# The first two weight tiles behind four LayerNorms are multiplied by the un-normalised input

## The chip, the cores and the metric

The kernel runs on one core of a Trainium2 chip. The time is that of one execution on the device, in microseconds (us); the median of three runs stands for the kernel. TensorE multiplies, VectorE, ScalarE and GpSimd (POOL in the profile) do the elementwise work, SyncE (SP) issues the loads of the weights.

## The reference, cut to what matters

A model of two blocks in fp32: 512 positions, width 1024. The first block has two layers of attention and FFN; the second starts with a LayerNorm, and each of its two layers is a token mixer, a LayerNorm, a convolutional FFN and a LayerNorm. What is computed around the change:

```python
def layer_norm(x, g, b):
    mu = jnp.mean(x, axis=-1, keepdims=True)
    var = jnp.mean(jnp.square(x - mu), axis=-1, keepdims=True)
    return (x - mu) * lax.rsqrt(var + EPS) * g + b

def conv_ffn(h, w_up, w_dw, w_down):
    u = depthwise_conv(h @ w_up, w_dw)
    g, val = jnp.split(u, 2, axis=-1)
    return (jax.nn.silu(g) * val) @ w_down

def token_mixers(h, ...):
    proj = h @ w_in          # 20 tiles of 128 columns here
    ...                      # short convolution, gated linear attention (a scan), latent attention, 31-tap convolution
    return y @ w_out
```

`h` in `h @ w_up` and `h @ w_in` is the output of a LayerNorm. Four of the five LayerNorms of the second block are followed by such a product.

## The kernel before

Activations lie transposed, 128 channels on the partitions by 512 positions, so the hidden state is eight slices `h[k]` of 128x512. To keep fp32 precision every product is three matmuls on rounded operands (`gemm`): `whi`·`n_hi` (L668), `whi`·`n_lo` (L669) and `wlo`·`n_hi` (L670). A tile is 128 output channels: eight slices of three matmuls for an input of 1024. Weights stream in: SyncE loads a tile into `raw`; ScalarE makes `whi` (`split_hi`, L639), GpSimd `wlo` = raw - whi (`split_lo`, L559). There are two result banks `bank_G`, two places each of `raw`, `whi` and `wlo`. ScalarE empties a bank (`take`, L645) and right behind it splits the tile two ahead, since that place is free then. So an engine that takes tile n late also lets tile n+2 start late.

The LayerNorms are objects of class `Norm`, `NORMS[0]` to `[4]`; the first four are "split", which means that their result is needed as `n_hi` and `n_lo` for a product. They stand behind the tile groups `down1b` (n = 0, "plain", a last RMS norm is folded in), `out2b` (1), `down2b` (2) and `out3b` (3). 0 and 2 lead into the mixer's input tiles `mix_in`, 1 and 3 (`narrow`) into the FFN's `up2a` and `up3a`. Behind each tile of the group VectorE adds the residual, subtracts a rough mean ("shift", L919), and ScalarE squares. `norm_tile_pe` sums over channels with matmuls by a matrix of ones: the first moment into `bank_O` (L792, the last part L827), the second into `bank_S` (L795, L829). Each call is two passes. When the last part is in, `norm_end_act` squares the mean (L864), takes Ln (L866) and Exp (L868), which gives the scale `rstd`; `norm_end_dve` centres the slices (L952), forms the variance (L966), and goes over the eight slices: norm (L977), centre of a slice four ahead, `n_lo` of the slice before (L956). ScalarE makes `n_hi` (L878) and adds the bias to `h` (L873).

TensorE starts the next group by `ramp_gemms_n`: the first two tiles slice by slice as each `n_lo` arrives, the second two slices behind; then `ramp_next_n`, the third tile in halves, whose halves of `whi` and `wlo` are made by themselves (L621, L627, L609, L612). In the FFN, VectorE then convolves gate and up (L1103, L1104, L1105 each), multiplies (`prod`, L1125) and makes `a_lo` (L1127), ScalarE applies silu (L1082) and makes `a_hi` (L1084), one chunk of a gate and an up tile at a time; `take` of the gate waits for the convolution of the chunk before, `take` of up for its product. In the mixer, tiles 0 and 1 and two small matmuls (AUP) feed the decay chain: `gate_in` (L2517, L2736), Exp and Ln (L2521, L2522), L2741, two scans (L2744), and then decays (L2269 to L2272), 31 taps (L2756) and mask copies (L2295) on VectorE, between which TensorE goes through the input tiles and, at L2221, the scan's matmuls. The order on each engine is the order of the code; engines meet only at semaphores.

## Time and profile before

| | us |
|---|---|
| median of 3 runs (2587.82 to 2592.54) | 2589.61 |
| the profiled execution | 2590.14 |
| its span | 2588.2 |
| TensorE busy | 2481.5 |
| VectorE busy | 1719.8 |
| ScalarE busy | 1024.9 |
| GpSimd busy | 958.2 |

The span is the time from the first to the last instruction that the profiler saw; 1.9 us of the profiled execution lie around it. The mean granted clock of TensorE over the span is 0.985 of full. Busy shares are means over the span; where an engine stands still, and for whom, is told by the rows below.

### The profile page before, as it was taken

What the parts mean: (1) busy time and instruction counts of PE and PEld (TensorE: products, weight loads), DVE (VectorE), ACT (ScalarE), POOL (GpSimd) and SP (SyncE); (2) the same over time, 40 slices, a digit from 0 to 9 for tenths busy, and PEclk for the clock granted to TensorE, in tenths of its full rate; (3) what the DMA queues carried; (4) which work ended last, traced back from release to release, by engine and by line L of the source; (5) the groups of instructions that cost most, each with busy time, mean ns of one, the idle gap of its engine ahead of it and who ended that gap; (6) DMA issues with size and microseconds to landing.
All of it is one profiled execution on the core that took longest, in us unless ns stands there. A gap on an engine that the chain in (4) does not pass through costs nothing.

```text
span 2588.2 us, 33451 instructions
## 1 busy us (share of the span) xinstructions
PE 2481.5 (96%) x11222; PEld 1907.6 (74%) x11222; DVE 1719.8 (66%) x2281; ACT 1024.9 (40%) x1623; POOL 958.2 (37%) x391
## 2 busy tenths in 40 slices
PE   7999999999999999999899889999989988999997
PEld 5676787888777688888676467788767746778876
DVE  7654774587777777276787667718668755781875
ACT  4444432232344532123554644313345454431333
POOL 2222444444310044444263034444435403453452
PEclk9999999999999999999999999999999999999999
DMA  5212232232332223223222022322322202232222
GB/s 171 78 58 61 86 97 90 89 100 95 102 92 74 74 89 101 90 94 106 67 90 62 13 66 85 105 86 89 104 77 83 66 8 74 81 98 89 94 97 77
DMA packets 65342, 217.48 MB, mean 84 GB/s; under 512 B 8416, under 2 KB 8672, under 8 KB 65120
## 3 DMA queue, kind: packets, MB, share of 16 engines
q1 hardware_dynamic: 64384, 214.79, 25.8%
q10 hardware_dynamic: 864, 1.44, 0.2%
q8 instruction: 58, 0.95, 0.2%
q14 instruction: 36, 0.29, 0.0%
HBM read 207.81 MB, written 2.10 MB: 81 GB/s over the span
## 4 chain that ended last, share of the span: by engine, by line
PE 78%; DVE 9%; issue 6%; ACT 3%; POOL 2%; DMA 0%; DVEq 0%; SPq 0%; ACTq 0%; POOLq 0%
PE bank_G L668 23%; PE bank_G L670 23%; PE bank_G L669 23%; POOL wlo L559 2%; DVE conv_up L1105 2%; DVE prod L1125 1%; ACT whi L639 1%; DVE h L952 1%; PE bank_S L1705 1%; PE bank_S L2221 1%; PE bank_X L1733 1%; PE bank_O L1957 1%; PE bank_O L1719 1%; PE bank_S L1946 1%; DVE conv_up L1104 1%
## 5 line engine op out<-in xcount | busy, mean ns | idle before, releaser
L559 POOL TENSOR_TENSOR wlo<-raw,whi 128x1024 fp32r<-128x1024 f32 (+2 forms) x361 | 905.3, 2509 | 1518.1 <-ACT whi L639 1493.0
L668 PE MATMUL bank_G<-n_hi,whi 128*128 128x512 f32 x2248 | 903.8, 402 | 49.3 <-DVE n_lo L956 27.2
L669 PE MATMUL bank_G<-n_lo,whi 128*128 128x512 f32 x2248 | 880.9, 392 | 0.0
L670 PE MATMUL bank_G<-n_hi,wlo 128*128 128x512 f32 x2248 | 880.8, 392 | 0.0
L639 ACT ACTIVATE whi<-raw 128x1024 fp32r<-128x1024 f32 (+2 forms) x389 | 403.4, 1038 | 603.8 <-PE bank_G L670 603.6
L668 PEld LDWEIGHTS bank_G<-n_hi,whi 128*128 128x128 f32 x2248 | 425.3, 189 | 168.7 <-DVE n_lo L956 36.3
L670 PEld LDWEIGHTS bank_G<-n_hi,wlo 128*128 128x128 f32 x2248 | 425.3, 189 | 91.3
L669 PEld LDWEIGHTS bank_G<-n_lo,whi 128*128 128x128 f32 x2248 | 425.9, 189 | 88.2 <-issue 4.8
L668 PE MATMUL bank_G<-a_hi,whi 128*128 128x512 f32 x704 | 277.9, 395 | 9.1 <-DVE a_lo L1127 3.9
L669 PE MATMUL bank_G<-a_lo,whi 128*128 128x512 f32 x704 | 275.2, 391 | 0.0
L670 PE MATMUL bank_G<-a_hi,wlo 128*128 128x512 f32 x704 | 275.0, 391 | 0.0
L668 PEld LDWEIGHTS bank_G<-a_hi,whi 128*128 128x128 f32 x704 | 132.8, 189 | 42.6 <-DVE a_lo L1127 7.3
L1105 DVE SCALAR_TENSOR_TENSOR conv<-gate,vec,conv 128x512 f32<-128x512 f32 x88 | 147.4, 1675 | 13.4 <-DVE conv L1104 7.6
L669 PEld LDWEIGHTS bank_G<-a_lo,whi 128*128 128x128 f32 x704 | 132.9, 189 | 28.0 <-issue 0.7
L670 PEld LDWEIGHTS bank_G<-a_hi,wlo 128*128 128x128 f32 x704 | 132.9, 189 | 27.9
L1024 DVE SCALAR_TENSOR_TENSOR h<-h,bank_G 128x512 f32 x32 | 21.9, 687 | 190.6 <-PE bank_G L670 190.6
L1887 DVE TENSOR_TENSOR h<-h,bank_G 128x512 f32<-128x512 f32 x80 | 54.9, 686 | 137.0 <-PE bank_G L670 136.9
L1125 DVE TENSOR_TENSOR prod<-silu,up 128x512 f32<-128x512 f32 x44 | 112.8, 2564 | 35.8 <-ACT silu L1073 35.8
L1105 DVE SCALAR_TENSOR_TENSOR conv_up<-up,vec,conv_up 128x512 f32<-128x512 f32 x44 | 112.6, 2559 | 6.4
L1127 DVE TENSOR_TENSOR a_lo<-prod,a_hi 128x512 f32 x88 | 60.9, 692 | 80.2 <-ACT a_hi L1084 40.1
L1101 DVE TENSOR_SCALAR conv<-gate,vec 128x512 f32<-128x512 f32 x44 | 98.1, 2229 | 10.2 <-DVE gate L655 10.2
L1104 DVE SCALAR_TENSOR_TENSOR conv<-gate,vec,conv 128x512 f32<-128x512 f32 x88 | 92.2, 1048 | 13.4 <-DVE conv L1101 7.0
(333 smaller groups left out, 2681.9 us busy)
## 6 DMA issues: line engine op xcount, KB each, us to landing
raw<-in_w_mix_in SPq DMA_DIRECT2D x40, 512.0 KB, 3.3
raw<-in_w_hyb_in SPq DMA_DIRECT2D x25, 512.0 KB, 3.4
raw<-in_w_diff_in SPq DMA_DIRECT2D x24, 512.0 KB, 3.3
raw<-in_w_up0a SPq DMA_DIRECT2D x22, 512.0 KB, 3.3
raw<-in_w_up0b SPq DMA_DIRECT2D x22, 512.0 KB, 3.3
raw<-in_w_up1a SPq DMA_DIRECT2D x22, 512.0 KB, 3.3
raw<-in_w_up1b SPq DMA_DIRECT2D x22, 512.0 KB, 3.3
raw<-in_w_up2a SPq DMA_DIRECT2D x22, 512.0 KB, 3.3
```

The source lines that it names most:

```text
L559: pool.tensor_tensor(b.wlo[:, g.slot, w], b.raw[:, g.slot, w], b.whi[:, g.slot, w], ALU.subtract).then_inc(b.lo_ready, 1)
L639: act.activation(b.whi[:, g.slot, w], b.raw[:, g.slot, w], ACT.Copy).then_inc(b.hi_ready, 1)
L668: pe.matmul(out, b.whi[:, g.slot, w], hi[:, hi_at + k, :], start=(k == 0), stop=False)
L669: pe.matmul(out, b.whi[:, g.slot, w], lo[:, lo_at + k, :], start=False, stop=False)
L670: mm = pe.matmul(out, b.wlo[:, g.slot, w], hi[:, hi_at + k, :], start=False, stop=(k == pieces - 1))
L952: dve.scalar_tensor_tensor(h[k], b.O[:, 0, :], -1.0 / D, h[k], ALU.mult, ALU.add).then_inc(b.centred, 1)
L1101: link(dve.tensor_scalar(dst[:, :], src[:, s:s + T], v_(b, w, c), v_(b, bias, c), ALU.mult, ALU.add))
L1104: link(dve.scalar_tensor_tensor(dst[:, :], src[:, s + 1:s + 1 + T], v_(b, w, FC + c), dst[:, :], ALU.mult, ALU.add))
L1105: return dve.scalar_tensor_tensor(dst[:, :], src[:, s + 2:s + 2 + T], v_(b, w, 2 * FC + c), dst[:, :], ALU.mult, ALU.add)
L1125: dve.tensor_tensor(b.prod[:, :], b.silu[:, :], up, ALU.mult).then_inc(b.prod_done, 1)
L1127: dve.tensor_tensor(b.a_lo[:, bass.ds(i, 1), :].rearrange("p a t -> p (a t)"), b.prod[:, :], b.a_hi[:, bass.ds(i, 1), :].rearrange("p a t ...
L1887: dve.tensor_tensor(h, h, b.G[:, g.slot, :], ALU.add).then_inc(b.evacuated, 1)
```

## The change

Normalising is linear: with x the shifted, un-normalised state, W'(((x - m)·s)·g + b) = s·(W'(x·g) - m·W'g) + W'b. The first two tiles (`EARLY = 2`) behind each split LayerNorm are now multiplied by x·g, before the moments are known, and corrected afterwards. The parts:

- ScalarE copies x·gain as `early_hi` behind each slice's square, VectorE makes the low half (L1073), in the tiles of the group before; they lie in buffers of their own (`early_ffn`, `early_mix`).
- TensorE forms W'g and W'b by a matmul with two moving columns, gain and bias, and the raw fp32 weights as the stationary operand (L892), eight for each early tile: those of the first inside the last product of the group, those of the second inside the first early tile. The moment matmuls go between the slices of the first early tile (`norm_sums_pe`).
- The scale is written to `bank_S` in PSUM, not to `rstd`. The rough mean is read from PSUM by VectorE without a copy by ScalarE.
- ScalarE copies the sums to `wcol`, makes mean × W'g for both tiles (L981) and adds W'b at the end (L986); VectorE adds the bank and multiplies by the scale (L1117, L1119), behind the second and the fifth norm. The low halves come two slices behind the norm, not one.
- The ramp is made of tiles 2 and 3, and tile 4 is the one in halves. `take` of tile 2 waits for the first convolution, of tile 3 for the first product (`after_early`).
- In the mixer the AUP matmuls come before the ramp, the bias copies of `gate_in` among the `n_hi`; the takes of tiles 2 and 3 stand ahead of the Exp and Ln of the decay chain. The mixer's small weights are loaded on ScalarE's queue before the last down group, not at the mixer's start.

```diff
+def early_split_lo(pool, b, name, m):
+    if m == 1:
+        pool.wait_ge(b.shifted, 8 * RAMPS.index(name) + 8)
+    if m == 2 * EARLY:
+        ramp_lo(pool, b, name)
+    else:
+        split_lo(pool, b, Index(FIRST[name] + m), W8)
...
-    g0 = FIRST[name]
+    g0 = FIRST[name] + EARLY
...
         self.shifts = {3: (0, 1, 2), 4: (3, 4)} if self.narrow else {3: (0, 1, 2, 3), 4: (4,)}
         self.shifts |= {5: (5,), 6: (6,), 7: (7,)}
+        self.lows = {4: (0,), 5: (1, 2), 6: (3,)} if self.narrow else {4: (0, 1), 5: (2, 3), 6: (4, 5)}
+        self.lows |= {7: range(4 if self.narrow else 6, KD)}
...
+def norm_sums_pe(pe, b, x, step):
+    if x.narrow:
+        if step == 0:
+            pe.wait_ge(b.shift_summed, x.added("q3"))
+            moment_pe(pe, b, x, 1, b.ntmp[:, 0])
+            pe.wait_ge(b.shift_summed, x.added("q5"))
+            moment_pe(pe, b, x, 0, b.rstd[:, :])
+        if step == 1:
+            moment_pe(pe, b, x, 1, b.ntmp[:, 1])
+            pe.wait_ge(b.shifted, 8 * x.n + 7)
+            moment_pe(pe, b, x, 0, b.h[:, 6, :])
+        if step == 2:
+            pe.wait_ge(b.shift_squared, 8 * x.n + 7)
+            moment_pe(pe, b, x, 1, b.mixed[:, 1])
+    elif step == 1:
+        if x.plain:
+            pe.wait_ge(b.plain_summed, 6)
+            pe.matmul(b.O[:, 1, :], b.k["ones"], b.mixed[:, 1], start=True, stop=False)
+        pe.wait_ge(b.shift_summed, x.added("q6"))
+        moment_pe(pe, b, x, 0, b.acc[:, :], True)
+        moment_pe(pe, b, x, 1, b.mixed[:, 0], True)
+    if step != 3:
         return
...
     pe.wait_ge(b.shifted, 8 * x.n + 8)
-    pe.matmul(b.O[:, 0, :], b.k["ones"], b.h[:, 7, :], start=False, stop=True).then_inc(b.first_moment, 1)
+    moment_pe(pe, b, x, 0, b.h[:, 7, :], stop=True).then_inc(b.first_moment, 1)
     pe.wait_ge(b.shift_squared, 8 * x.n + 8)
-    pe.matmul(b.S[:, 1, :], b.k["ones"], square_at(b, x, 7), start=False, stop=True).then_inc(b.second_moment, 1)
+    moment_pe(pe, b, x, 1, square_at(b, x, 7), stop=True).then_inc(b.second_moment, 1)
...
+def gain_sums_pe(pe, b, x, j, part):
+    g = Index(FIRST[x.ramp] + j)
+    for k in part:
+        if k == 0:
+            pe.wait_ge(loaded_at(b, g), loaded_count(g))
+            if j == 0:
+                free_bank(pe, b, x.w_at)
+                wait(pe, b.w_taken, x.n)
+        mm = pe.matmul(b.X[:, x.w_at.slot, 2 * j:2 * j + 2], b.raw[:, g.slot, k * P:(k + 1) * P], x.gain_and_bias(b, k),
+                       start=(k == 0), stop=(k == KD - 1))
+        if k == KD - 1:
+            mm.then_inc(b.w_summed, 1)
+def last_product_after(pe, b, x, pieces):
+    per = -(-KD // pieces)
+    return lambda k: gain_sums_pe(pe, b, x, 0, range(min(KD, k * per), min(KD, (k + 1) * per)))
+def early_pe(pe, b, x):
+    g0, (hi, lo) = FIRST[x.ramp], x.early(b)
+    def after(k):
+        gain_sums_pe(pe, b, x, 1, range(k, k + 1))
+        norm_sums_pe(pe, b, x, k)
+    gemm(pe, b, Index(g0), hi, lo, KD, lambda k: pe.wait_ge(b.early_lo, KD * x.n + k + 1), after=after)
+    gemm(pe, b, Index(g0 + 1), hi, lo, KD)
 def norm_products_pe(pe, b, x, hi, lo, pieces, ready):
     for m in range(KD):
-        gemm(pe, b, Index(x.g0 + m), hi, lo, pieces, ready if m == 0 else None)
-        norm_tile_pe(pe, b, x, m)
+        last = x.split and m == KD - 1
+        gemm(pe, b, Index(x.g0 + m), hi, lo, pieces, ready if m == 0 else None,
+             after=last_product_after(pe, b, x, pieces) if last else None)
+        norm_part_pe(pe, b, x, m)
+    if x.split:
+        early_pe(pe, b, x)
...
+        if x.split:
+            act.activation(x.early(b)[0][:, k, :], b.h[:, k, :], ACT.Copy, scale=v_(b, x.gain, k)).then_inc(b.early_hi, 1)
+def scale_of(b):
+    return b.S[:, 0, :]
...
     act.wait_ge(b.first_moment, n + 1)
     act.activation(b.acc[:, :], b.O[:, 0, :], ACT.Square, scale=1.0 / D).then_inc(b.moment_squared, 1)
+    if x.split:
+        act.wait_ge(b.centred, 8 * n + AHEAD[0])
+        act.activation(b.mean[:, :], b.O[:, 0, :], ACT.Copy, scale=-1.0 / D).then_inc(b.mean_taken, 1)
     act.wait_ge(b.variance_ready, n + 1)
     act.activation(b.rstd[:, :], b.rstd[:, :], ACT.Ln, bias=b.zero if x.plain else b.eps2).then_inc(b.scale_ready, 1)
     act.wait_ge(b.scale_ready, 2 * n + 1)
-    act.activation(b.rstd[:, :], b.rstd[:, :], ACT.Exp, scale=-0.5).then_inc(b.scale_ready, 1)
+    act.activation(scale_of(b), b.rstd[:, :], ACT.Exp, scale=-0.5).then_inc(b.scale_ready, 1)
+    if x.split:
+        act.wait_ge(b.w_summed, EARLY * (n + 1))
+        sums = b.X[:, x.w_at.slot, 0:2 * EARLY]
+        act.activation(b.wcol[:, 0:EARLY], sums[:, 0:2 * EARLY:2], ACT.Copy)
+        act.activation(b.wcol[:, EARLY:], sums[:, 1:2 * EARLY:2], ACT.Copy).then_inc(b.w_taken, 1)
+        act.wait_ge(b.w_taken, n + 1)
+        for j in range(EARLY):
+            act.activation(x.first_tile(b, j), b.mean[:, :], ACT.Copy, scale=b.wcol[:, j:j + 1]).then_inc(b.early_mean, 1)
+    def early_take(j):
+        y = x.first_tile(b, j)
+        act.wait_ge(b.early_tmp, 2 * (EARLY * n + j + 1))
+        act.activation(y, y, ACT.Identity, bias=b.wcol[:, EARLY + j:EARLY + j + 1]).then_inc(b.evacuated, 1)
...
+            if k == 0:
+                early_take(0)
+                split_hi(act, b, Index(FIRST[x.ramp] + EARLY))
+            if k == 3:
+                split_hi(act, b, Index(FIRST[x.ramp] + EARLY + 1))
+            if k == 4:
+                early_take(1)
+            if k == 5 and not x.narrow:
+                gate_copies_act(act, b, n // 2)
             if k >= 2:
                 biased(k - 2)
         else:
...
-        dve.tensor_tensor(h[k], h[k], b.mean[:, :], ALU.subtract).then_inc(b.shifted, 1)
+        dve.scalar_tensor_tensor(h[k], b.S[:, 0, :], -1.0 / (2 * P), h[k], ALU.mult, ALU.add).then_inc(b.shifted, 1)
...
+    if x.split:
+        for k in x.lows.get(m, ()):
+            dve.wait_ge(b.early_hi, KD * n + k + 1)
+            dve.scalar_tensor_tensor(x.early(b)[1][:, k, :], h[k], v_(b, x.gain, k), x.early(b)[0][:, k, :], ALU.mult,
+                                     ALU.subtract).then_inc(b.early_lo, 1)
...
         centre(k)
+    def norm(k):
+        dve.wait_ge(b.centred, 8 * n + k + 1)
+        dve.scalar_tensor_tensor(h[k], h[k], v_(b, x.gain, k), scale_of(b), ALU.mult, ALU.mult).then_inc(b.normed, 1)
+    def correct(j):
+        g, y = Index(FIRST[x.ramp] + j), x.first_tile(b, j)
+        dve.wait_ge(b.early_mean, EARLY * n + j + 1)
+        dve.wait_ge(b.gemm_done, g.n + 1)
+        dve.tensor_tensor(y, y, b.G[:, g.slot, :], ALU.add).then_inc(b.early_tmp, 1)
+        dve.wait_ge(b.early_tmp, 2 * (EARLY * n + j) + 1)
+        dve.tensor_tensor(y, y, scale_of(b), ALU.mult).then_inc(b.early_tmp, 1)
+    if x.narrow:
+        for y in (b.gate, b.up):
+            dve.memset(y[:, 0:PAD], 0.0).then_inc(b.padded, 1)
+            dve.memset(y[:, PAD + T:], 0.0).then_inc(b.padded, 1)
     dve.wait_ge(b.scale_ready, 2 * n + 2)
     for k in range(KD):
-        dve.wait_ge(b.centred, 8 * n + k + 1)
-        dve.scalar_tensor_tensor(h[k], h[k], v_(b, x.gain, k), b.rstd[:, :], ALU.mult, ALU.mult).then_inc(b.normed, 1)
+        norm(k)
         if k + AHEAD[1] < KD:
             centre(k + AHEAD[1])
-        if x.split and k:
-            low(k - 1)
+        if not x.split:
+            continue
+        if k == 1:
+            correct(0)
+        if k == 4:
+            correct(1)
+        if k >= 2:
+            low(k - 2)
     if x.split:
+        low(KD - 2)
         low(KD - 1)
...
+    def after_early():
+        act.wait_ge(b.conv_done, c0 + 1)
+        take(act, b, Index(g0 + 2), b.gate[:, PAD:PAD + T], ramp=True)
+        act.activation(b.silu[:, :], b.conv[:, :], ACT.Silu).then_inc(b.silu_done, 1)
+        act.wait_ge(b.prod_done, c0 + 1)
+        take(act, b, Index(g0 + 3), b.up[:, PAD:PAD + T], width=W8)
+        act.activation(b.a_hi[:, 0, :], b.prod[:, :], ACT.Copy).then_inc(b.act_hi, 1)
+        act.wait_ge(b.conv_done, c0 + 2)
+        act.activation(b.silu[:, :], b.conv[:, :], ACT.Silu).then_inc(b.silu_done, 1)
+        act.wait_ge(b.prod_done, c0 + 2)
+        act.activation(b.a_hi[:, 1, :], b.prod[:, :], ACT.Copy).then_inc(b.act_hi, 1)
+    if name in RAMPS:
+        after_early()
...
             free_bank(pe, b, p)
             pe.matmul(b.X[:, p.slot, :], b.aup[rows, :], b.mx[rows, M_GA, :], start=True, stop=True).then_inc(b.posted, 1)
-    ramp_next_n(pe, b, f"mix_in{l}", gate_up)
-    for m in range(3, SCAN_TILE):
+    gate_up()
+    ramp_gemms_n(pe, b, f"mix_in{l}", 48 + 24 * l)
+    ramp_next_n(pe, b, f"mix_in{l}")
+    for m in range(2 * EARLY + 1, SCAN_TILE):
         tile(m)
...
+def mixer_weights_act(act, b, l, mixw):
     if l:
         act.wait_ge(b.headed, HEADS0[3])
+    act.dma_start(b.aup[:, :], mixw[l, :, 10 * P:11 * P]).then_inc(b.mix_w_in, 16)
     act.dma_start(b.uq[:, :, :], mixw[l, :, 0:6 * P].rearrange("p (k m) -> p k m", k=2)).then_inc(b.mix_w_in, 16)
     act.dma_start(b.ukv[:, :], mixw[l, :, 6 * P:10 * P]).then_inc(b.mix_w_in, 16)
...
-        take(act, b, Index(g0 + m), b.mx[:, m, :], GLA_DK ** -0.5 if m == M_GQ else 1.0, ramp=m == 0)
-    act.wait_ge(b.evacuated, g0)
-    tile(0)
-    tile(1)
-    for d in range(2):
...
+        take(act, b, Index(g0 + m), b.mx[:, m, :], GLA_DK ** -0.5 if m == M_GQ else 1.0, ramp=m == EARLY)
+    tile(2)
+    tile(3)
     x = b.gate_in[:, 2:4, :]
     act.wait_ge(b.gate_abs, l + 1)
     link(act.activation(x, x, ACT.Exp, scale=-1.0))
     act.activation(x, x, ACT.Ln, bias=b.one).then_inc(b.gate_log, 1)
-    tile(2)
-    act.wait_ge(b.evacuated, g0 + M_GATE + 2)
+    tile(4)
     for j in range(2):
         y = b.mx[:, M_GATE + j, :]
...
```

TensorE behind the LayerNorm of `out2b`, from the last product of the group. `ntmp`, `rstd`, `h`, `mixed` and `sq` are sources of moment calls, `const` the ones. Before:

```order
L670 MATMUL bank_G<-n_hi,wlo 128x512
L795 MATMUL bank_S<-ntmp,const 128x512
L792 MATMUL bank_O<-rstd,const 128x512
L795 MATMUL bank_S<-ntmp,const 128x512
L792 MATMUL bank_O<-h,const 128x512
L795 MATMUL bank_S<-mixed,const 128x512
L827 MATMUL bank_O<-h,const 128x512
L829 MATMUL bank_S<-sq,const 128x512
L668 MATMUL bank_G<-n_hi,whi 128x512
```

and now:

```order
L892 MATMUL bank_X<-vec,raw 128x2 x2
L694 MATMUL bank_G<-early_ffn_61,whi 128x512
L695 MATMUL bank_G<-early_ffn_62,whi 128x512
L696 MATMUL bank_G<-early_ffn_61,wlo 128x512
L892 MATMUL bank_X<-vec,raw 128x2
L836 MATMUL bank_S<-ntmp,const 128x512
L836 MATMUL bank_O<-rstd,const 128x512
L694 MATMUL bank_G<-early_ffn_61,whi 128x512
L695 MATMUL bank_G<-early_ffn_62,whi 128x512
L696 MATMUL bank_G<-early_ffn_61,wlo 128x512
L892 MATMUL bank_X<-vec,raw 128x2
L836 MATMUL bank_S<-ntmp,const 128x512
```

The calls of the moments, which stood in one row, are now spread over the slices of a tile that works on the early buffers, with the two-column calls between.

VectorE at the end of the same LayerNorm. Before:

```order
L952 SCALAR_TENSOR_TENSOR h<-bank_O,h 128x512
L966 SCALAR_TENSOR_TENSOR rstd<-bank_S,acc 128x512
L952 SCALAR_TENSOR_TENSOR h<-bank_O,h 128x512 x3
L977 SCALAR_TENSOR_TENSOR h<-h,vec,rstd 128x512
L952 SCALAR_TENSOR_TENSOR h<-bank_O,h 128x512
L977 SCALAR_TENSOR_TENSOR h<-h,vec,rstd 128x512
L952 SCALAR_TENSOR_TENSOR h<-bank_O,h 128x512
L956 SCALAR_TENSOR_TENSOR n_lo<-h,vec,n_hi 128x512
L977 SCALAR_TENSOR_TENSOR h<-h,vec,rstd 128x512
L952 SCALAR_TENSOR_TENSOR h<-bank_O,h 128x512
L956 SCALAR_TENSOR_TENSOR n_lo<-h,vec,n_hi 128x512
```

and now:

```order
L1124 MEMSET gate 128x2
L1123 MEMSET up 128x2
L1124 MEMSET up 128x2
L1111 SCALAR_TENSOR_TENSOR h<-h,vec,bank_S 128x512
L1084 SCALAR_TENSOR_TENSOR h<-bank_O,h 128x512
L1111 SCALAR_TENSOR_TENSOR h<-h,vec,bank_S 128x512
L1084 SCALAR_TENSOR_TENSOR h<-bank_O,h 128x512
L1117 TENSOR_TENSOR gate<-gate,bank_G 128x512
L1119 TENSOR_TENSOR gate<-gate,bank_S 128x512
L1111 SCALAR_TENSOR_TENSOR h<-h,vec,bank_S 128x512
L1084 SCALAR_TENSOR_TENSOR h<-bank_O,h 128x512
L1088 SCALAR_TENSOR_TENSOR n_lo<-h,vec,n_hi 128x512
```

The first low half of the normalised slices comes behind the third norm where it came behind the second, and the correction of the gate tile stands ahead of it.

ScalarE at the start of the FFN behind it. Before:

```order
L621 ACTIVATE whi<-raw 128x512
L873 ACTIVATE h<-h,vec 128x512 x2
L645 ACTIVATE gate<-bank_G 128x512
L627 ACTIVATE whi<-raw 128x512
L645 ACTIVATE up<-bank_G 128x512
L639 ACTIVATE whi<-raw 128x1024
L1082 ACT_TABLE_LOAD
L1082 ACTIVATE silu<-conv 128x512
L1084 ACTIVATE a_hi<-prod 128x512
```

and now:

```order
L647 ACTIVATE whi<-raw 128x512
L991 ACTIVATE h<-h,vec 128x512 x2
L671 ACTIVATE gate<-bank_G 128x512
L653 ACTIVATE whi<-raw 128x512
L1248 ACT_TABLE_LOAD
L1248 ACTIVATE silu<-conv 128x512
L671 ACTIVATE up<-bank_G 128x512
L665 ACTIVATE whi<-raw 128x1024
L1251 ACTIVATE a_hi<-prod 128x512
L1253 ACTIVATE silu<-conv 128x512
L1255 ACTIVATE a_hi<-prod 128x512
```

The take of `up` has moved behind the first silu, and the high half of the second chunk's product ahead of the loop.

## Rows read from the trace of the kernel before

**Rows 1.** Page, busy time of the engines, and the costliest group of GpSimd (busy, mean ns)

```profile
PE 2481.5 (96%) x11222; PEld 1907.6 (74%) x11222; DVE 1719.8 (66%) x2281; ACT 1024.9 (40%) x1623; POOL 958.2 (37%) x391
...
L559 POOL TENSOR_TENSOR wlo<-raw,whi 128x1024 fp32r<-128x1024 f32 (+2 forms) x361 | 905.3, 2509 | 1518.1 <-ACT whi L639 1493.0
```

**Rows 2.** Waits of TensorE: us in total, times, longest us

```profile
PE bank_G L668 <- DVE n_lo L956: 27.2, 12, 6.9
```

**Rows 3.** Timeline of TensorE behind `out2b`: start us, us, what [idle before <- releaser]

```profile
1531.02 1.02 PE L795 MATMUL bank_S<-ntmp,const 128*128 128x512 f32 x2
...
1535.31 1.02 PE L827 MATMUL bank_O<-h,const 128*128 128x512 f32 x2
...
1543.39 0.79 PE L668 MATMUL bank_G<-n_hi,whi 128*128 128x512 f32 x1 [6.20 <-DVE n_lo L956]
...
1571.02 0.49 PE L668 MATMUL bank_G<-n_hi,whi 128*128 128x512 f32 x1 [1.46 <-POOL wlo L559]
...
1582.03 0.39 PE L668 MATMUL bank_G<-n_hi,whi 128*128 128x512 f32 x1
```

**Rows 4.** Windows: us, busy of PE, PEld, DVE, ACT, POOL, clock, DMA share, GB/s

```profile
1543.00:1550.00 7.00, 6.06 (x13) 3.84 (x14) 7.00 (x12) 4.79 (x8) 0.00 (x0) 0.50 0.00 0
1440.00:1444.00 4.00, 1.30 (x6) 0.42 (x4) 3.63 (x9) 1.09 (x4) 0.00 (x0) 1.00 0.02 9
1444.00:1450.00 6.00, 3.65 (x5) 1.59 (x6) 3.22 (x8) 3.48 (x8) 0.00 (x0) 0.57 0.00 0
```

**Rows 5.** Timeline of VectorE behind `out2b`, to the product of the FFN's second chunk

```profile
1540.08 0.74 DVE L977 SCALAR_TENSOR_TENSOR h<-h,vec,rstd 128x512 f32<-128x512 f32 x1
...
1551.74 1.63 DVE L956 SCALAR_TENSOR_TENSOR n_lo<-h,vec,n_hi 128x512 fp32r<-128x512 f32 x2
...
1557.52 0.49 DVE L1103 TENSOR_SCALAR conv<-gate,vec 128x512 f32<-128x512 f32 x1 [3.75 <-ACT gate L645]
...
1560.61 2.62 DVE L1103 TENSOR_SCALAR conv_up<-up,vec 128x512 f32<-128x512 f32 x1
...
1565.15 0.69 DVE L1125 TENSOR_TENSOR prod<-silu,conv_up 128x512 f32<-128x512 f32 x1
...
1575.90 0.69 DVE L1125 TENSOR_TENSOR prod<-silu,conv_up 128x512 f32<-128x512 f32 x1
```

**Rows 6.** Timeline of ScalarE, then of GpSimd, at the same place

```profile
1539.15 0.63 ACT L868 ACTIVATE rstd<-rstd 128x512 f32<-128x512 f32 x1
...
1566.90 1.05 ACT L639 ACTIVATE whi<-raw 128x1024 fp32r<-128x1024 f32 x1
...
1560.48 2.47 POOL L559 TENSOR_TENSOR wlo<-raw,whi 128x1024 fp32r<-128x1024 f32 x1 [1.24 <-ACT whi L639]
```

**Rows 7.** The chain that ended last (eight transposes), and TensorE by line (busy, mean ns)

```profile
75.08 1.02 PE bank_X L1733 x8
...
L1914 PE MATMUL bank_S<-lamp,const 64*128 64x2 f32 x2 | 0.4, 258 | 0.0
...
L668 PEld LDWEIGHTS bank_G<-n_hi,whi 128*128 128x128 f32 x2248 | 425.3, 189 | 168.7 <-DVE n_lo L956 36.3
```

**Rows 8.** Timelines of TensorE and VectorE in the first mixer of the second block

```profile
1263.86 1.02 PE L808 MATMUL bank_O<-mixed,const 128*128 128x512 f32 x2
...
1268.20 1.12 PE L827 MATMUL bank_O<-h,const 128*128 128x512 f32 x2 [0.75 <-DVE h L919]
...
1301.24 1.22 DVE L2741 TENSOR_TENSOR gate_in<-gate_in 128x1024 f32<-128x1024 f32 x1 [1.59 <-ACT gate_in L2522]
...
1305.95 0.50 PE L668 MATMUL bank_G<-n_hi,whi 128*128 128x512 f32 x1 [1.43 <-POOL wlo L559]
...
1308.20 2.61 DVE L2270 TENSOR_TENSOR decayed<-ntmp 128x256 f32<-128x256 f32 x1
...
1349.47 1.34 DVE L2295 COPY_PREDICATED scores_t<-glmask,bank_X 128x512 f32<-128x512 uint8 x2
...
1350.95 0.38 PE L2221 MATMUL bank_S<-const 32*128 32x128 f32 x2
```

166 lines of the change are left out of this document (92 added, 74 removed).

## The prediction

> **What bounds the kernel now.** I read the page first: TensorE is busy for 2481.5 us of the 2588.2 us span, VectorE for 1719.8 us [rows 1]. Little can be won but where TensorE stands still, so the next view is that of its waits. Its longest from one cause is on `n_lo` ahead of a tile, 27.2 us over 12 waits, the longest 6.9 us [rows 2]: four LayerNorms, each with one long and some short waits. The timeline of TensorE around one of them (behind `out2b`) has the pattern [rows 3]. The last product of the group ends where the first moment matmul starts, at 1531.02; I call this E. The last part of the first moment starts at 1535.31, 4.3 us later, and the next tile only at 1543.39, after 6.20 us of idling. In the windows view the idling has a sequel: from 1543 to 1550 TensorE is granted 0.50 of its clock (1.2 GHz, half of 2.4) [rows 4]. The place thus costs 6.20 us, and half of the 7 us at half clock, 3.5 us. Over four places that would be 39 us, the most that the change could bring if TensorE alone set the end. It does not do so here: behind the LayerNorm, VectorE's convolution [rows 5] and the loop take, weight split, product [rows 6] go on without slack. So I follow VectorE and ask when it comes to its next piece of the chain.
>
> **FFN places (LN behind `out2b` and `out3b`), step by step from E.**
>
> *TensorE to the first moment.* Before: E+4.3. After, in program order: 8 two-column calls ahead of E's end, then four early slices of three matmuls, four two-column calls, five moment calls. A slice is .68 us and a moment call .86, since those before start at 1531.02 and 1535.31 with five between the two [rows 3]. No two-column call of 128 rows by raw fp32 weights is in the trace. The nearest are the fp32 transposes, 8 in 1.02 us, .13 each, and a 64-row call of two, 258 ns for both, .13 each [rows 7]. The calls take two passes each. I take .13 a pass, .26 a call; the bounds are 0 (wholly hidden beside the neighbours) and .19 a pass, the mean of a weight load of the products [rows 7]. The sum is 8 × .26 + 4 × (.68 + .26) + 5 × .86 = 2.1 + 3.8 + 4.3 = 10.2 us. First moment at E+10.2 where it was E+4.3: **+5.9 us**.
>
> A page weighs on this price by a sentence that my sum does without: the Trainium skill, "TensorE: Matmul & The Clock Gate", section "LDWEIGHTS (loading the stationary operand)", lets a load of 128 columns cost about 107 ns at any number of moving columns; by that, an estimate, 24 passes ahead of the moment would make the place 0.55 us cheaper.
>
> *To the first norm.* The chain square, variance, Ln, Exp, norm took from 1535.31 by Exp at 1539.15 to the norm at 1540.08 [rows 3, 5, 6], 4.8 us. It stays, with four memsets (.5 us) and the wait for ScalarE's copy of the mean (some .1) ahead of the first norm: about 1546.6.
>
> *VectorE's own work.* Before, 8 norms, 4 centres and 8 low halves took from 1540.08 to 1553.37, 13.3 us for 20 instructions, .66 each [rows 5]. After, four correction instructions join (.62 each, like the .69 us products of [rows 5], 2.5 us), inside that row. Now a new neighbour: GpSimd's split of the third tile's `wlo`, which waits for ScalarE's `whi` behind the first `n_hi`, falls from about 1552.1 to 1554.6 into the low halves. Beside such a split (2.47 us, at 1560.48) VectorE's L1103 took 2.62 us instead of .49 [rows 5, 6], 2.1 more. I count one such stretch, at 1.8 us, since part of the split lies beside a norm. Sum 13.3 + 2.5 + 1.8 = 17.6, less .2 since it overlaps the end: last low half at 1564.0, **+10.6 us** against 1553.4. Bounds of the stretch: 0 and 2 × 2.1.
>
> The Trainium skill, "SBUF — State Buffer", on the port pair that VectorE and GpSimd share, has an operation with two SBUF inputs fully blocked by a GpSimd read, and one with at most one (the other in PSUM) free. By that the low halves are stretched, while the norms, whose scale now lies in PSUM, are not; no row of before has a low half beside GpSimd. If it doesn't hold for them, the sum is 1.8 us less a place, 2594.
>
> *What the early tiles give back.* Before, VectorE then waited 3.75 us for the gate tile, and its first convolution began at 1557.52 and the product at 1565.15, 7.6 us later, the stretched L1103 (2.1 us too long) among it [rows 5]. After, both tiles of chunk 0 lie corrected in SBUF, so it begins at once, at 1564.0; only splits of half a tile lie beside it, for which I put .4 in place of the 2.1, 5.9 us: product at **1569.9, +4.8 us**. Chunk 1: its gate is taken before the product, but `up` only behind it; then `a_hi`, a low half stretched by GpSimd, and the convolution: second product 1579.7 against 1575.9, **+3.8 us**. Only then does ScalarE free the bank of the seventh tile, split its weights (1.05 us [rows 6]) and GpSimd the low half (2.5 us [rows 1]): the tile starts at 1585.1 against 1582.03 [rows 3], **+3.0 us**. From there each chunk of two tiles follows the last in the same loop as before, whose links (take, split, low split, product) leave TensorE no room to catch up; the shift stays to the end of the group.
>
> *TensorE meanwhile.* It works from E through two early tiles to 1552.4, idles 2.5 us and again 2.7 us (low halves), and is ahead at its fifth tile, 1568.2 against 1571.02 [rows 3]; but then it idles about 5 us before the seventh. A clock of 0.57 followed 4 us of which TensorE was busy for 1.30 [rows 4], and 0.50 followed the 6.20. If the 5 us have that sequel, it costs up to 3.5 us more. So +3 without, +6.5 with it; I take the middle: **+4.5 us each, +9 for both**.
>
> **Mixer places (LN behind `down1b` and `down2b`).** From E=1263.86 the last part of the first moment started 4.3 us later, at 1268.20 [rows 8]; after, 2.1 + 3.8 and four other calls of .86 with no gap between, E+9.2: +4.9. TensorE's fifth tile was at 1305.95 [rows 8] and comes at about 1300.0, −6. But the mixer's decay chain on VectorE starts with L2741 at 1301.24 [rows 8] after ScalarE's Exp and Ln. These stand now behind the takes of tiles 2 and 3; the last of them is at 1300.4, and L2741 comes at 1304.1: **+2.9**. What VectorE owes from here is the bound: its four mask copies end at 1350.81, and the scan matmuls that read them start at 1350.95 [rows 8]. TensorE's lead of 6 us ends there. Against the +2.9: some instructions of 256 columns took 2.6 us, L2270 at 1308.20 among them, where 1024 columns took 1.22 [rows 8]; they lay beside GpSimd's splits, which come earlier now. Two may come free, some 4.4 us. Bounds −1.5 and +3; I take **+1 each, +2 for both**.
>
> **Hidden at no price.** The mean shift without its ScalarE copy and the early halves on ScalarE (8 × .7 us) and VectorE (8 × .66, half of them ahead of E) go beside the last products. If they are late, TensorE waits in the early slices (case D). The mixer's weight DMAs move from the mixer's start to before the last down group: aup is wanted tens of us later. GpSimd's first early tile has its split before E; the second waits for the last shift, as before.
>
> **Sum.** 9 + 2 = +11 us on the profiled 2590.14 us gives 2601.1; the median is .5 lower, 2589.61: I say **2601.0**. At 0 a pass it is 4 × 3.1 less (2589), at .19 a pass 4 × 1.4 more (2607); without the stretches 4 × 1.8 less.
>
> **Rivals.**
> - *A, the forecast:* own range 2590 to 2614, chance .58, of which .16 lies within 0.2%.
> - *B1, TensorE's lead is kept throughout* (faster). If chunk loops and scan have slack that I do not see, each place gives its lead: 2 × 3 and 2 × 6 us, 2572. For it: TensorE 96% busy [rows 1]. Against: the convolution waits for its tile and the scan matmuls start .14 us behind the mask copies [rows 5, 8]. Decides if VectorE reaches the mask copies 2.9 us or more before TensorE. .08.
> - *B2, the lead is kept in the mixers alone:* 2 × −6 + 2 × 3 = −6, 2584. The escape from GpSimd speaks for it. .16 (.12 faster, .04 same).
> - *C, gaps with sequel in the clock, at all four places:* 2 × 6.5 + 2 × (2.9 + 3.5) = +26, 2616. .10.
> - *D, it doesn't do what it says:* the early low halves, four of them behind the last shift on VectorE (2.6 us), hold TensorE and so the moments: +2.6 each on A, 2611. .08.
>
> **Numbers.** 0.2% is 5.2 us, about what a measurement of this kernel can tell. Faster .08 + .12 = .20; same .16 + .04 = .20; slower .42 + .10 + .08 = .60. From 2582 to 2614 B1 and most of C are left out, under .2; the ends take in the prices of a pass.
>
> **What would show it.** In the profile after: two-column calls at a pitch of .26; the last moment part at E+10; no idle of 6 us before the first tile but gaps of 2.5 us at the third; the last `n_lo` 10 us later; the product of chunk 0 near E+39, of chunk 1 near E+49; a gap of 5 us before the seventh tile; L2741 3 us later against E. Wrong it would be if TensorE's seventh tile starts earlier against E than before, if the granted clock stays 1.00, or if the scan matmuls start earlier.

## The result, and the profile after

| | before | after |
|---|---|---|
| median, us | 2589.90 (2587.82 to 2592.54) | 2614.58 (2609.39 to 2618.33) |
| profiled execution, us | 2590.14 | 2617.62 |
| its span, us | 2588.2 | 2615.8 |

The ratio is 1.0108, with a 95% interval from 1.0081 to 1.0134: slower by 24.7 us. I had said 2601.0, with 2614.0 as the upper end. The sign was right, the size (11.4 us) was less than half of what came. The kernel before is itself spread: in later sessions its executions took 2579 to 2593 us, with a mean of 2585 to 2587, so the profiled one, 2590.14, lies near their upper end, and the profiled one of after lies 3.0 us above its median.

Where it went can be read without a model. Both kernels issue the same 9240 product matmuls (L668 to L670 before, L694 to L696 after) in the same order. Take the n-th of each and subtract its start from that of before: the difference is the lag. Read in quiet stretches between the places, it is -1.2 us ahead of the first LayerNorm, +5.1 behind the first mixer, +12.1 behind the FFN, +22.1 behind the second mixer and +27.7 behind the second FFN. So the four places cost **+6.3, +7.0, +9.9 and +5.6 us**: the two mixers 16.2, the two FFNs 12.6. This compares one execution with one other.

The page, and the waits of TensorE (us in total, times, longest):

```profile
PE 2497.6 (95%) x11350; PEld 1925.8 (74%) x11350; DVE 1761.6 (67%) x2329; ACT 1048.2 (40%) x1670; POOL 966.4 (37%) x391
...
PE bank_G L694 <- POOL wlo L576: 24.8, 29, 5.1
...
PE bank_S L2400 <- DVE scores_t L2474: 9.0, 5, 2.9
...
PE bank_G L694 <- DVE n_lo L1088: 7.6, 4, 2.3
...
PE bank_S L2400 <- ACT scores_t L2425: 5.6, 2, 2.9
```

The wait on `n_lo` fell from 27.2 to 7.6 us [rows 2], so the change does what it says. But GpSimd's low halves are now waited for up to 5.1 us at a time, and the waits of the scan matmuls on VectorE's mask copies and on ScalarE's copies (both write `scores_t`) are new.

**The FFN place behind `out2b`.** TensorE first, then VectorE and GpSimd, timeline of the kernel after (start us, us, what [idle before <- releaser]); the last product's end, E, is 1536.0, which is 1537.79, the start of the first early slice, less eight two-column calls of .22:

```profile
1535.14 0.50 PE L892 MATMUL bank_X<-vec,raw 128*128 128x2 f32 x4
1535.51 0.47 PE L694 MATMUL bank_G<-n_hi,whi 128*128 128x512 f32 x1
1535.82 0.39 PE L695 MATMUL bank_G<-n_lo,whi 128*128 128x512 f32 x1
...
1545.74 1.10 PE L836 MATMUL bank_O<-h,const 128*128 128x512 f32 x2
...
1558.94 0.47 PE L694 MATMUL bank_G<-n_hi,whi 128*128 128x512 f32 x1 [2.12 <-issue]
...
1562.86 0.79 PE L694 MATMUL bank_G<-n_hi,whi 128*128 128x512 f32 x1 [1.60 <-DVE n_lo L1088]
...
1591.22 0.79 PE L694 MATMUL bank_G<-n_hi,whi 128*128 128x512 f32 x1 [5.07 <-POOL wlo L576]
```

```profile
1550.79 0.74 DVE L1111 SCALAR_TENSOR_TENSOR h<-h,vec,bank_S 128x512 f32<-128x512 f32 x1
...
1556.54 0.75 DVE L1111 SCALAR_TENSOR_TENSOR h<-h,vec,bank_S 128x512 f32<-128x512 f32 x1
...
1557.80 1.60 DVE L1088 SCALAR_TENSOR_TENSOR n_lo<-h,vec,n_hi 128x512 fp32r<-128x512 f32 x1
...
1566.03 2.06 DVE L1088 SCALAR_TENSOR_TENSOR n_lo<-h,vec,n_hi 128x512 fp32r<-128x512 f32 x3
...
1575.51 0.69 DVE L1299 TENSOR_TENSOR prod<-silu,conv_up 128x512 f32<-128x512 f32 x1 [2.22 <-ACT silu L1248]
...
1585.37 0.69 DVE L1299 TENSOR_TENSOR prod<-silu,conv_up 128x512 f32<-128x512 f32 x1
...
1556.49 2.35 POOL L576 TENSOR_TENSOR wlo<-raw,whi 128x1024 fp32r<-128x1024 f32 x1 [13.83 <-ACT whi L665]
```

The windows over the gap and behind it (us, busy of PE, PEld, DVE, ACT, POOL, granted clock, DMA share, GB/s):

```profile
1584.00:1590.00 6.00, 2.15 (x10) 1.45 (x8) 4.61 (x7) 3.49 (x5) 1.69 (x1) 1.00 0.00 0
1590.00:1596.00 6.00, 4.78 (x11) 3.79 (x12) 5.65 (x4) 0.63 (x1) 3.86 (x2) 0.53 0.43 125
```

| from E, us | before [rows 3, 5] | forecast | after |
|---|---|---|---|
| last part of the first moment | 4.3 | 10.2 | 9.7 |
| first norm | 9.1 | 15.6 | 14.8 |
| last low half ready | 22.4 | 33.0 | 32.1 |
| product of chunk 0 | 34.1 | 38.9 | 39.5 |
| product of chunk 1 | 44.9 | 48.7 | 49.4 |
| seventh tile | 51.0 | 54.1 | 55.2 |

The working of this place held step by step to about 1 us, with the 5 us gap ahead of the seventh tile and the granted clock of 0.53 (nearer 1.2 GHz than 2.4) behind it.

The price of the place was still above the forecast, and the reason lies further up than the seventh tile. TensorE had idled 2.12 us ahead of its third tile, and its clock fell there too. The third tile therefore ended late, ScalarE's take of it waited 3.14 us on TensorE, the first silu stood behind this take and a table load, and VectorE waited 2.22 us for the silu. In e12 below, whose code is the same here, the clock was down for a shorter time, the take waited for VectorE and not for TensorE, and VectorE did not wait for the silu (its product began at 1569.66, when the silu had ended at 1569.56). ScalarE's take and the windows behind the first gap, first in the kernel after, then in e12, where E is 4.7 us earlier:

```profile
1572.41 0.60 ACT L671 ACTIVATE gate<-bank_G 128x512 f32<-128x512 f32 x1 [3.14 <-PE bank_G L696]
...
1561.00:1564.00 3.00, 1.40 (x4) 0.95 (x4) 3.00 (x4) 1.92 (x4) 1.26 (x1) 0.50 0.42 119
1564.00:1567.00 3.00, 3.00 (x10) 2.33 (x9) 3.00 (x6) 3.00 (x6) 0.00 (x0) 0.59 0.40 146
...
1566.50 0.60 ACT L671 ACTIVATE gate<-bank_G 128x512 f32<-128x512 f32 x1 [1.91 <-DVE conv L1279]
...
1554.00:1557.00 3.00, 2.73 (x6) 1.84 (x6) 2.97 (x5) 2.62 (x5) 1.97 (x2) 0.53 0.47 175
1557.00:1560.00 3.00, 1.99 (x9) 1.51 (x9) 3.00 (x4) 2.29 (x4) 0.58 (x1) 0.90 0.38 102
```

The lag of the seventh tile within the place is +4.1 us in the kernel after and +3.0 in e12; one tile later it is +7.0 and +4.5.

**The first mixer.** VectorE, then GpSimd and TensorE, timeline of the kernel after (here E is 1263.4: the start of the last tile of `down1b` and the length that this tile had before, so that the two-column calls inside it count as after E):

```profile
1305.23 1.33 DVE L2914 TENSOR_TENSOR gate_in<-gate_in 128x1024 f32<-128x1024 f32 x1 [6.29 <-ACT gate_in L2698]
...
1317.75 2.58 DVE L2451 TENSOR_TENSOR const<-ntmp 128x256 f32<-128x256 f32 x1
1320.55 5.35 DVE L2945 TENSOR_TENSOR cpad<-mx 128x512 f32<-128x512 f32 x2 [0.22 <-DVE const L2451]
...
1339.79 2.60 DVE L2449 TENSOR_TENSOR decayed<-ntmp 128x256 f32<-128x256 f32 x1
...
1354.54 1.33 DVE L2474 COPY_PREDICATED scores_t<-glmask,bank_X 128x512 f32<-128x512 uint8 x2
...
1317.67 2.37 POOL L576 TENSOR_TENSOR wlo<-raw,whi 128x1024 fp32r<-128x1024 f32 x1 [6.38 <-ACT whi L665]
1320.01 2.56 POOL L2673 TENSOR_TENSOR decayed<-decayed,mx 128x1024 f32<-128x1024 f32 x1
1322.52 2.82 POOL L576 TENSOR_TENSOR wlo<-raw,whi 128x1024 fp32r<-128x1024 f32 x1
...
1346.30 0.38 PE L2400 MATMUL bank_S<-const 32*128 32x128 f32 x2 [2.73 <-ACT scores_t L2425]
```

L2914, the old L2741, comes at E+41.8 where it came at E+37.4 [rows 8]. The first four mask copies end at E+92.4, where they ended at E+86.9. GpSimd now goes from one instruction into the next for four instructions from 1317.67 on, and both `cpad` products lie beside it: 5.35 us for two. In the kernel before only one of the two lay beside GpSimd (2.77 us). In this mixer 6 instructions of VectorE of some 2.6 us stand where there were 3, in the second one 9 where there were 4. Each of these 22 ends 0.28 to 0.55 us behind the end of a GpSimd instruction beside it, which is why I call them collisions. The second mixer shows what follows; TensorE at five scan matmuls, some 10 us apart:

```profile
2008.95 0.38 PE L2400 MATMUL bank_S<-const 32*128 32x128 f32 x2 [2.88 <-ACT scores_t L2425]
...
2018.82 0.38 PE L2400 MATMUL bank_S<-const 32*128 32x128 f32 x2 [1.45 <-DVE scores_t L2474]
...
2028.63 0.38 PE L2400 MATMUL bank_S<-decayed 32*128 32x128 f32 x2 [2.95 <-DVE scores_t L2474]
...
2037.43 0.58 PE L2400 MATMUL bank_S<-decayed 32*128 32x128 f32 x2 [1.95 <-DVE scores_t L2474]
...
2047.20 0.38 PE L2400 MATMUL bank_S<-const 32*128 32x128 f32 x2 [1.33 <-DVE scores_t L2474]
```

None of these waits is there in the kernel before. I call such a row a cascade.

### The profile page after: what moved, and what is told of

Same layout as the page of the kernel before. It is cut to its first block, busy times and chain, and to the rows that moved or that the text cites. A ratio compares the mean times of both kernels' runs of the same rounds, so it can differ in the third digit from the quotient of the medians.

```text
span 2615.8 us, 33724 instructions
## 1 busy us (share of the span) xinstructions
PE 2497.6 (95%) x11350; PEld 1925.8 (74%) x11350; DVE 1761.6 (67%) x2329; ACT 1048.2 (40%) x1670; POOL 966.4 (37%) x391
## 4 chain that ended last, share of the span: by engine, by line
PE 74%; DVE 13%; issue 7%; ACT 3%; POOL 2%; DVEq 1%; DMA 0%; ACTq 0%; POOLq 0%; SPq 0%
PE bank_G L694 22%; PE bank_G L696 21%; PE bank_G L695 21%; POOL wlo L576 2%; DVE conv_up L1279 2%; ACT whi L665 1%; DVE prod L1299 1%; PE bank_S L1884 1%; PE bank_X L1912 1%; DVE h L1084 1%; PE bank_O L2136 1%; PE bank_O L1898 1%; PE bank_S L2125 1%; DVE n_lo L1088 1%; DVE bank_O L2929 1%
## 5 line engine op out<-in xcount | busy, mean ns | idle before, releaser
L694 PE MATMUL bank_G<-n_hi,whi 128*128 128x512 f32 x2184 | 881.5, 404 | 46.7 <-POOL wlo L576 21.2
L696 PE MATMUL bank_G<-n_hi,wlo 128*128 128x512 f32 x2184 | 858.5, 393 | 0.0
L695 PE MATMUL bank_G<-n_lo,whi 128*128 128x512 f32 x2184 | 858.0, 393 | 0.0
L694 PEld LDWEIGHTS bank_G<-n_hi,whi 128*128 128x128 f32 x2184 | 414.9, 190 | 159.5 <-issue 41.6
L696 PEld LDWEIGHTS bank_G<-n_hi,wlo 128*128 128x128 f32 x2184 | 414.5, 190 | 89.6
L695 PEld LDWEIGHTS bank_G<-n_lo,whi 128*128 128x128 f32 x2184 | 415.5, 190 | 86.7 <-issue 5.1
L694 PE MATMUL bank_G<-a_hi,whi 128*128 128x512 f32 x704 | 279.0, 396 | 9.9 <-DVE a_lo L1301 3.9
L696 PE MATMUL bank_G<-a_hi,wlo 128*128 128x512 f32 x704 | 274.8, 390 | 0.0
L694 PEld LDWEIGHTS bank_G<-a_hi,whi 128*128 128x128 f32 x704 | 132.6, 188 | 43.2 <-DVE a_lo L1301 7.2
L696 PEld LDWEIGHTS bank_G<-a_hi,wlo 128*128 128x128 f32 x704 | 132.5, 188 | 28.0
L1275 DVE TENSOR_SCALAR conv<-gate,vec 128x512 f32<-128x512 f32 x44 | 98.1, 2229 | 10.2 <-DVE gate L681 10.2
```

The source lines that it names most:

```text
L694: pe.matmul(out, b.whi[:, g.slot, w], hi[:, hi_at + k, :], start=(k == 0), stop=False)
L695: pe.matmul(out, b.whi[:, g.slot, w], lo[:, lo_at + k, :], start=False, stop=False)
L696: mm = pe.matmul(out, b.wlo[:, g.slot, w], hi[:, hi_at + k, :], start=False, stop=(k == pieces - 1))
L1275: link(dve.tensor_scalar(dst[:, :], src[:, s:s + T], v_(b, w, c), v_(b, bias, c), ALU.mult, ALU.add))
```

## The experiments

The places of all runs, as lags between the same matmuls, in the one execution that was profiled; "long" is the number of VectorE instructions of 1.9 to 3 us (mask copies and scans left out) in the two mixers; "chain" is the start of L2741 or L2914 after E. Some expectations put a place or E by up to 2 us otherwise (4.7 and 9.5 us for the two mixers of the kernel after, E+42.5 for its chain); the table reads all runs in one way. The ratio is to the kernel before, from all timed runs.

| run | mixer 1 | FFN 1 | mixer 2 | FFN 2 | long | chain | ratio (95%) |
|---|---|---|---|---|---|---|---|
| before | 0 | 0 | 0 | 0 | 3, 4 | 37.4, 34.9 | 1 |
| after | +6.3 | +7.0 | +9.9 | +5.6 | 6, 9 | 41.8, 39.5 | 1.0108 (1.0081 to 1.0134) |
| e1 | +3.5 | +4.6 | +1.1 | +4.2 | 5, 5 | 37.6, 35.3 | 1.0068 (1.0052 to 1.0085) |
| e2 | +7.8 | +3.4 | +9.2 | +3.0 | 7, 9 | 41.4, 37.7 | 1.0101 (1.0077 to 1.0125) |
| e3 | +14.9 | +2.7 | +6.2 | +2.8 | 10, 7 | 41.9, 39.9 | 1.0065 (1.0048 to 1.0082) |
| e4 | +3.1 | +3.2 | +2.4 | +2.8 | 5, 5 | 40.3, 39.5 | 1.0106 (1.0084 to 1.0128) |
| e5 | +3.6 | -0.1 | +6.6 | 0.0 | 5, 7 | 37.6, 33.8 | 1.0020 (1.0006 to 1.0035) |
| e6 | +0.4 | -1.9 | -2.5 | +0.2 | 3, 4 | 40.2, 36.8 | 1.0006 (0.9993 to 1.0019) |
| e7 | +3.2 | +2.6 | +0.3 | +2.7 | 5, 5 | 37.6, 35.2 | 1.0054 (1.0035 to 1.0073) |
| e8 | +3.5 | -0.8 | -0.3 | -0.6 | 5, 5 | 37.5, 33.8 | 1.0025 (1.0012 to 1.0038) |
| e9 | -1.5 | +0.1 | -5.0 | +0.1 | 3, 3 | 37.6, 33.8 | 0.9999 (0.9985 to 1.0013) |
| e10 | -1.3 | 0.0 | -5.1 | +0.2 | 3, 3 | 37.6, 33.8 | 1.0008 (0.9991 to 1.0025) |
| e11 | 0.0 | 0.0 | -0.1 | 0.0 | 3, 4 | 37.4, 34.9 | 1.0000 (0.9986 to 1.0013) |
| e12 | +0.3 | +4.4 | -2.1 | +4.2 | 2, 3 | 41.8, 39.5 | 1.0042 (1.0024 to 1.0061) |
| e13 | +0.3 | +3.2 | -3.6 | +2.9 | 2, 3 | 41.8, 39.5 | 1.0031 (1.0017 to 1.0046) |
| e14 | -1.2 | +7.0 | -4.1 | +5.7 | 3, 3 | 37.6, 35.2 | 1.0041 (1.0021 to 1.0061) |
| e15 | +0.5 | -1.0 | -5.0 | -0.5 | 3, 3 | 37.6, 33.8 | 0.9979 (0.9968 to 0.9990) |

How far can one execution mislead? e11 gives 0.0, 0.0, -0.1 and 0.0, but e6 has -1.9 in the first FFN, where its code is that of the kernel before: the granted clock over the 22 us from E was 0.84 in e6 and 0.77 in the kernel before.

```profile
1531.00:1553.00 22.00, 15.25 (x39) 8.77 (x38) 17.17 (x27) 14.16 (x20) 4.65 (x2) 0.77 0.15 48
...
1528.00:1550.00 22.00, 15.25 (x46) 8.90 (x45) 16.79 (x26) 13.74 (x20) 4.66 (x2) 0.84 0.15 48
```

My theory at the start was that ScalarE's order delays VectorE's decay chain in the mixer, and that the late moment and the clock make the FFN's price. The rival in the mixer was that only the collisions of VectorE with GpSimd count.

**e1, ScalarE's Exp and Ln first.**

```diff
-    tile(2)
-    tile(3)
     x = b.gate_in[:, 2:4, :]
     act.wait_ge(b.gate_abs, l + 1)
     link(act.activation(x, x, ACT.Exp, scale=-1.0))
     act.activation(x, x, ACT.Ln, bias=b.one).then_inc(b.gate_log, 1)
+    tile(2)
+    tile(3)
```

> Against the changed kernel, whose first mixer place costs 4.7 us and the second 9.5 by the trace. Edit: in the mixer, ScalarE's Exp and Ln of the decay gates stand ahead of the takes of tiles 2 and 3. Theory (ScalarE's order delays VectorE's decay chain): L2914 comes 3.5 to 4 us earlier against E, the scan matmuls too, at both places, so 7 to 8 us less: some 2607. Rival (what sets the end of the scan is how often VectorE lies beside GpSimd's splits): L2914 earlier by the same, but the scan matmuls by less than 1.5 us, total within 3 us of 2614.6. Third case: the later takes of tiles 2 and 3 hold TensorE at tiles 4 and 5; then the time is the same or longer.

The chain came 4.2 us earlier at both places and the time fell by 0.40%, 10 us, more than either expectation. But the masks of the first mixer ended only 2.5 us earlier (E+89.9), and the number of long instructions fell as well, so this run does not part the two theories.

**e2, the moments first.**

```diff
-    def after(k):
-        gain_sums_pe(pe, b, x, 1, range(k, k + 1))
-        norm_sums_pe(pe, b, x, k)
+    for step in range(4):
+        norm_sums_pe(pe, b, x, step)
+    gain_sums_pe(pe, b, x, 1, range(KD))
...
-        if k == 1:
+        if k == 3:
             correct(0)
-        if k == 4:
+        if k == 6:
             correct(1)
```

> Edit: all moment matmuls stand ahead of the first early slice, the two-column sums of the second early tile right behind them, and the two corrections come behind the fourth and seventh norm (takes and splits on ScalarE moved with them). Theory (the late moment is what delays VectorE): last part of the first moment at E+6.1 instead of E+9.7 behind out2b, last low half 3.5 us earlier against E, and all four places cheaper by about 3.5: some 2600. Rival (VectorE's and GpSimd's later work would be late anyhow, or the early tile now arrives too late for the correction): last low half earlier by less than 1.5 us, or a new wait of VectorE on bank_G ahead of the correction, total 2610 to 2615.

The last part of the first moment came at 1543.21, 6.1 us after E, and both FFN places fell by about 3 us (7.0 to 3.4, 5.6 to 3.0). In the mixers it did nothing: 7 and 9 long instructions, cascade and all. A miss for "all four places".

**e3, silu first.**

```diff
         act.wait_ge(b.conv_done, c0 + 1)
-        take(act, b, Index(g0 + 2), b.gate[:, PAD:PAD + T], ramp=True)
         act.activation(b.silu[:, :], b.conv[:, :], ACT.Silu).then_inc(b.silu_done, 1)
+        take(act, b, Index(g0 + 2), b.gate[:, PAD:PAD + T], ramp=True)
         act.wait_ge(b.prod_done, c0 + 1)
-        take(act, b, Index(g0 + 3), b.up[:, PAD:PAD + T], width=W8)
         act.activation(b.a_hi[:, 0, :], b.prod[:, :], ACT.Copy).then_inc(b.act_hi, 1)
+        take(act, b, Index(g0 + 3), b.up[:, PAD:PAD + T], width=W8)
```

> Edit: at the start of the FFN behind a split LayerNorm, ScalarE's first silu (with its table load) stands ahead of the take of tile 2, and the first a_hi ahead of the take of tile 3. Theory (VectorE's waits of 2.2 us on silu and 2.3 us on a_hi are handed on to the seventh tile): product of chunk 0 2 us earlier, of chunk 1 3 us earlier, seventh tile 3 us earlier, 6 us less in all: some 2609. Rival (the later take of tile 2 delays the second half of tile 4, and the gap before tile 7 only moves): seventh tile within 1 us, total within 2 us.

The seventh tile's lag in the place fell from 4.1 to 1.3 us, as expected; about 1.1 us of that is the clock behind the first gap, since e1, e4 and e12, without this edit, have 3.0. The mixers, whose code is that of the kernel after, cost +14.9 and +6.2 in this trace, against +6.3 and +9.9: with the same instructions they vary by many microseconds, and so does the number of their long instructions. The traced execution, 2618.12 us, was the slowest of five; the other four took 2599 to 2603.

**e4, TensorE kept busy ahead of the seventh tile.**

```diff
         gemm_n(pe, b, Index(g0 + 2 * EARLY + 1))
+        for _ in range(19):
+            pe.matmul(b.S[:, 1, :], b.n_hi[:, 0, 0:P], b.n_hi[:, 1, :], start=True, stop=True)
         done = 2 * EARLY + 2
```

> Edit: 19 extra matmuls (128x512, sources n_hi, result unused) stand on TensorE ahead of the seventh tile in the two FFNs behind a split LayerNorm, where it idles for 5.1 us; 19 x .2265 = 4.3 us, so that they end before the tile may start. Their result is used by nothing. Theory (the gap lowers the granted clock, and that costs 3 us a place): the clock stays at 1.00 after the seventh tile's start, seventh tile at the same time against E, 12th matmul behind it 3 us earlier, 5 to 6 us less in all: some 2609. Rival (the clock falls for another reason, or the loop's links on VectorE take back what the clock gives): clock down in the same stretch, or up and the total within 2 us of 2614.6.

The granted clock behind the seventh tile stayed at 1.00 and the FFN places cost 3.2 and 2.8. The total did not show it. The traced execution, 2601.66 us, was the fastest of four (the others 2607 to 2616), so its mixers, +3.1 and +2.4, do not speak for the others; that the mixers took the rest is argued, not shown.

**e5, e1 to e3 together; e7, e1 and e3; e8, e5 with the matmuls of e4.**

> The three edits of e1, e2 and e3 together on the changed kernel. Behind out2b the seventh tile started 4.1 us later against E in the changed kernel, 1.3 later with the moments first, 1.2 later with silu first. If the two act on the same chain (product of chunk 0 and 1 on VectorE), both add: seventh tile 1.5 us earlier than before, each FFN place at -1 to +1. Mixers: decay chain (L2914) at about E+36 at the first, where before had E+37.4, 4 or fewer stretched instructions of VectorE, no row of gaps; place 0 to +2. Total within 5 us of before. Rival (the corrections on VectorE, 2.5 us a place, cannot be won back by any order): FFN places stay at +2 to +3, mixers +2 to +4, total 8 to 12 us above before.

> The edits of e1 and e3 together on the changed kernel, moments left where the change put them. Theory (they act at different places and add): FFN places +2.7 each, mixer places +1 to +4 each, total 8 to 13 us above before. Rival (a cascade of gaps in the mixer depends on where VectorE stands against GpSimd, not on this order): a mixer place of +6 or more.

> e5 with the 19 extra matmuls of e4 ahead of the seventh tile (their result is used by nothing). If a gap of over 3 us stands there in e5 and the clock falls behind it, this is 1 to 3 us a place faster than e5. If the gap in e5 is shorter than the 4.3 us that they take, they delay the seventh tile by the difference and the total is 0 to 4 us longer than e5.

The FFN edits add, as expected: -0.1 and 0.0 in e5. Its mixers missed: +3.6 and +6.6 with 5 and 7 long instructions, where I had expected 0 to +2 with 4 or fewer. In e7 the FFN places came as expected (2.6 and 2.7), the total 14 us above before and not 8 to 13. The extra matmuls gave 0.7 and 0.6 us a place, below what was expected, and e5 and e8 have the same ratio within their intervals. In e5 the second mixer had a cascade (+6.6), in e8 with the same code none (-0.3).

**e6, the late chain alone, in the kernel before.**

```diff
+    tile(2)
+    link(act.activation(x, x, ACT.Copy))
     link(act.activation(x, x, ACT.Exp, scale=-1.0))
     act.activation(x, x, ACT.Ln, bias=b.one).then_inc(b.gate_log, 1)
-    tile(2)
```

> The kernel BEFORE with nothing of the change, but in the mixer ScalarE takes tile 2 and makes one extra copy of gate_in onto itself ahead of the Exp and Ln of the decay gates, so that VectorE's chain (L2741) starts some 4 us later against E, as in the changed kernel. Theory (the mixer places cost what they do since this chain is late, and lateness brings further collisions of VectorE with GpSimd and waits of TensorE): both mixer places cost 4 to 10 us, gaps of 2 to 3 us on TensorE at the scan matmuls, total 2596 to 2606. Rival (the cost comes from the early tiles and corrections themselves): each place costs less than 2 us, total within 4 us of before.

My theory fell. The chain came 2.8 and 1.9 us later (I had aimed at 4), the long instructions stayed at 3 and 4, the first masks ended at E+87.7, and the places cost +0.4 and -2.5. So lateness of this size is not the price by itself; it was less than the 4.4 and 4.6 us of the kernel after, so the run does not rule out a price of the rest. From here the rival, that what the chain meets is the price, was my theory.

**e9, e5 with the `cpad` products earlier; e10, with ScalarE's fifth Exp later; e11, both in the kernel before; e12, the first alone in the kernel after.** The edit of e9 and e12:

```diff
     for turn in range(4):
+        if turn == 2:
+            dve.wait_ge(b.evacuated, g0 + M_A + 2)
+            for j in range(2):
+                dve.wait_ge(b.sigmoided, 2 * l + j + 1)
+                link(dve.tensor_tensor(b.cpad[:, j, middle], b.mx[:, M_A + j, :], b.mx[:, M_GATE + j, :], ALU.mult))
         scan_decays_dve(dve, b, link, l, turn)
```

(the same two products are taken out behind the loop), and that which e10 adds, in `mixer_act`:

```diff
         if turn == 2:
             scan_copy_act(act, b, l, FAR[1], 1)
+            scan_exp_act(act, b, l, 4)
...
-        if turn + 3 < len(LEVELS):
+        if turn + 3 < len(LEVELS) and turn != 1:
             scan_exp_act(act, b, l, turn + 3)
```

> e5 with one more edit: VectorE makes the two cpad products behind the second group of decays, not behind the fourth. In e5 both lay beside GpSimd (2.6 and 2.7 us instead of .69) while GpSimd went from one split into the next. Theory (the mixer places cost what their extra collisions of VectorE with GpSimd cost, 1.9 to 2.2 us each): one or two stretched instructions fewer, mask copies 2 to 4 us earlier against E, the first mixer place at 0 to +1.5 where e5 had +3.6; total 3 to 6 us less than e5. Rival (whatever is moved meets another split, so that the number of collisions stays): cpad .69 each but as many others stretched, places unchanged.

> e9 with ScalarE's Exp of the fifth decay group moved behind the score copies of the next level. In e5 that Exp waited for VectorE and held the copies for which TensorE stood still for 2.9 us at E+81. Theory: this gap goes, each mixer place is 1 to 3 us cheaper than in e9, and the total is under that of before by 2 us or more. Rival (TensorE then waits for the mask copies instead, which are on the same VectorE): a gap of the same sum some us later, total within 1.5 us of e9.

> The kernel BEFORE with the two edits of e10 in the mixer and nothing of the change. In before only three instructions of VectorE are stretched there and TensorE has no gap at the scan matmuls. Expected if the edits only mend what the change broke: within 3 us of before. If they help by themselves: 2 to 6 us under before, and e10 must be compared with this kernel rather than with before.

> The changed kernel with the cpad edit alone. By the theory of collisions both mixer places lose 2 to 4 us and the row of gaps behind E+98 that the second had is gone or shorter, total 2604 to 2610. By the rival theory (the late decay chain of VectorE, E+42.5 instead of E+37.4, is the price and no collision): places fall by less than 1.5 us each, total 2612 or more.

e12 is the clearest run. Its chain is as late as in the kernel after (E+41.8, E+39.5), yet with two `cpad` products moved to where GpSimd rests the mixers, in its trace, cost +0.3 and -2.1 us and not +6.3 and +9.9. VectorE in its first mixer:

```profile
1306.53 1.33 DVE L2914 TENSOR_TENSOR gate_in<-gate_in 128x1024 f32<-128x1024 f32 x1 [6.34 <-ACT gate_in L2698]
...
1316.51 1.42 DVE L2925 TENSOR_TENSOR cpad<-mx 128x512 f32<-128x512 f32 x2 [0.23 <-DVE decayed L2451]
...
1318.98 2.59 DVE L2451 TENSOR_TENSOR const<-ntmp 128x256 f32<-128x256 f32 x1
...
1350.14 1.34 DVE L2474 COPY_PREDICATED scores_t<-glmask,bank_X 128x512 f32<-128x512 uint8 x2
```

The two products take 1.42 us, not 5.35, and the masks end 5.6 us earlier against E, at E+86.8, where they ended before the change. The ratio fell from 1.0108 to 1.0042, 17 us, more than the 5 to 11 that I had expected, and all six executions (2592 to 2604 us) lie under the fastest of the kernel after (2609). The clock is a rival for the mixers that the traces can settle. Both mixers in the kernel after, then in e12:

```profile
1265.00:1401.00 136.00, 126.29 (x778) 96.58 (x777) 114.77 (x166) 74.49 (x110) 69.14 (x28) 0.95 0.21 69
1932.00:2070.00 138.00, 121.78 (x763) 93.94 (x762) 118.32 (x159) 71.73 (x105) 67.60 (x28) 0.96 0.21 67
...
1265.00:1395.00 130.00, 124.65 (x778) 95.64 (x777) 109.44 (x166) 73.40 (x109) 64.81 (x28) 0.96 0.22 74
1925.00:2053.00 128.00, 122.68 (x772) 94.25 (x772) 105.93 (x162) 72.93 (x108) 66.18 (x28) 0.96 0.22 71
```

The granted clock is nearly the same; what differs is VectorE's busy time, less by 5.3 and 12.4 us. In the FFNs, whose code e12 does not touch, its places are lower by 2.6 and 1.4 us, and that is the clock of its one execution. The same edit, with that of e10, does nothing in the kernel before (e11, 1.0000): it mends what the change broke and is no gain by itself. e10 shows nothing beyond e9: TensorE's wait of 2.9 us at E+81 in e5, for which its edit was meant, is already gone in e9.

**e13, e12 with the matmuls of e4; e14, e12 with the edit of e1; e15, e9 with the matmuls of e4.**

> e12 (changed kernel, cpad products early, mixer places near 0 in its trace) with the 19 extra matmuls of e4 ahead of the seventh tile of both FFNs (result used by nothing). FFN places by the traces: +4.4 and +4.2 without them, +3.2 and +2.8 with them in e4. If the granted clock behind the gap is the difference: 1.2 to 1.4 us less a place, total 2 to 3 us less than e12. If the clock costs 3 us a place, as forecast: total 6 us less. If the loop on VectorE gives the tempo: no difference.

> e12 with the Exp and Ln ahead of the takes (the edit of e1). The decay chain then comes at E+38.3 instead of E+42.6. If lateness of the chain has a price apart from collisions: mixer places 2 to 4 us below those of e12, total 4 to 7 us less. If only collisions count: the places move by what the number of stretched instructions moves, 2 in e12; with 4 of them, as in e9, the gain is 0 to 2 us.

> e9 with the extra matmuls of e4. The gap ahead of the seventh tile is some 3 us here and they take 4.3, so each FFN place changes by +1.3 for the delay and -1.3 for the clock: total within 2 us of e9, and within 0.2% of before or just under it. It would be the fastest version if the mixer places keep -1.5 and -5.

TensorE's windows behind the gap in e12, and the same stretch in e13:

```profile
1580.00:1586.00 6.00, 0.93 (x4) 0.55 (x3) 4.88 (x6) 3.68 (x6) 3.55 (x2) 0.91 0.00 0
1586.00:1592.00 6.00, 6.00 (x23) 4.89 (x22) 4.49 (x4) 1.07 (x2) 2.01 (x1) 0.81 0.56 179
...
1580.00:1586.00 6.00, 5.18 (x23) 3.98 (x22) 4.88 (x6) 3.50 (x6) 3.39 (x2) 1.00 0.00 0
1586.00:1592.00 6.00, 6.00 (x28) 4.95 (x27) 4.70 (x4) 1.10 (x2) 2.22 (x1) 1.00 0.57 175
```

The seventh tile starts at the same lag in both (+3.0), and the place costs 4.4 without and 3.2 us with the matmuls. Over the tile behind the gap the lag grows by 1.5 us in e12 and by 0.1 in e13, so the clock behind this gap costs 1.4 us there. In e14, with the FFN code of e12, the place costs 7.0, as in the kernel after. Of the 2.6 us between them 1.1 are there when the seventh tile starts (+4.1), by the clock behind the first gap, and behind the seventh tile the lag grows by 2.9. So the clock behind the gap of 5 us costs 1.4 or 2.8 us, with the same code. The ratios of e13 and e12 (1.0031, 1.0042) differ by the 2 to 3 us that I had expected, but their intervals overlap.

e14 also bounds the price of a late chain without the `cpad` collisions: 1.5 and 2.0 us a mixer place, for 4.2 us of lateness. The granted clock over its mixers was 0.99 against 0.96 in e12, so a part of this can be the clock's. In the traces the FFN places took back what the mixers gave (7.0 and 5.7 against 4.4 and 4.2), and the total is that of e12; but two of its ten executions took 2610.6 and 2611.5 us, the other eight 2590 to 2600, and no trace shows what happened in those two.

e15 is faster than both kernels: 0.9979, with an interval that leaves out 1, 5.4 us under before. It came out as expected, just under before. It is the change with ScalarE's two orders turned round, the moments ahead, the `cpad` products early, and TensorE kept busy in the gap.

## Why the prediction was wrong

- *What bounds the kernel, and that a lead of TensorE is lost:* right. TensorE was ahead by 11.6 us at the first early matmul behind `down1b`, and both mixer places still ended behind. With the collisions gone they did not: e9 has -1.5 and -5.0 (granted clock over the two mixers 0.99, against 0.96 before), which is the side of case B2, though read against one execution of before.
- *TensorE to the first moment, +5.9:* +5.4. A two-column call costs .22: in the rows above, four passes and one product matmul take from 1535.14 to 1535.82, .68, less .2265 for the product (a third of a slice's .68), .11 a pass where I had taken .13. The Trainium skill ("TensorE: Matmul & The Clock Gate", "LDWEIGHTS (loading the stationary operand)") gives the load as the number of columns divided by 1.2, in ns; for 128 columns that is an estimate of 107 ns, and the trace's .11 agrees.
- *Last low half, +10.6:* +9.7. One low half took 1.60 us beside the split at 1556.49, while the norm at 1556.54, whose scale is in PSUM, took its .75 beside the same split. By the rule of the Trainium skill ("SBUF — State Buffer", "Who interferes with whom") the first, with two inputs in SBUF, is held and the second is not; the trace agrees with both halves.
- *The FFN places, +4.5 each:* in e12 this holds in both its parts, +3.0 to the seventh tile (forecast +3.0) and 1.4 for the clock behind it (forecast 1.5), and the places are 4.4 and 4.2. In the kernel after they were 7.0 and 5.6, around the 6.5 that I had as the upper end. I had put no clock behind the first gaps (forecast 2.5 and 2.7 us, measured 2.12 and 1.60); there it fell, in the first FFN of the kernel after for longer than in e12, and by way of the third tile, ScalarE's take, the table load and the silu this made VectorE wait 2.22 us and the seventh tile 1.1 us later still. Behind the seventh tile the clock cost 2.8 us, where I had taken half of 3.5. This term was short by 3.6 us in all.
- *The mixer places, +1 each:* this is the step that failed. They cost 6.3 and 9.9, 14.2 us more than the +2 for both. The lateness of the chain was forecast as 2.9 us and was 4.4, but e12, as late, shows that this is not the main price. I had written that collisions of VectorE with GpSimd "may come free", because GpSimd's splits come earlier now, and took the +1 from that. What came was the opposite, 6 and 9 long instructions for 3 and 4. Tiles run earlier against VectorE, so GpSimd's splits and its scan products close up into a row of four at the place where VectorE has its `cpad` products. A bound from below of -1.5 with +3 above was no bound: it had no term for more collisions, at 1.9 to 2.2 us each, nor for the waits of TensorE that they start.
- *Case C* had the right total, 2616, with a sum of 26 us, but its reason for the mixers, the clock, is not theirs: at nearly the same granted clock, with 2 and 3 collisions and none on `cpad`, e12 has them at +0.3 and -2.1. The right total of this case is luck. I had given it .10.
- *The range:* its upper end, 2614.0, lay 0.6 us under the median. With three more collisions in each mixer as the upper bound (+6) the upper end would have been 2620.

**Left open.** What decides in one execution whether the cascade starts isn't shown: with the same mixer code, places cost from 2.4 to 14.9 us (after, e3, e4). That the collisions of the `cpad` products feed it is shown by e9 and e12, in whose traces there is no cascade; that none occurs in the other timed executions of these kernels is not shown. e9's ratio of 0.9999 beside places that sum to -6.3 us is no sign of one: its traced execution, 2584.95 us, lies at its median, 2585.16, and the trace of before, with which the places compare, lies 3 to 5 us above that kernel's middle in the same session. Why the clock behind the same gap is down for a longer time in one execution than in another isn't shown.

## What to carry to other kernels

A step that makes the bound engine early also moves the engines that feed it; ask what their work now lies beside, and put an upper bound on added collisions as readily as on removed ones. Before trusting that an engine's lateness is the cost, delay it alone in the old kernel, and by as much as the change does. Where the same code gives places of 3 and 15 us in two executions, compare places in traces, and look where the traced execution lies among the timed ones before you take it for the kernel.

## What the runs showed of the hardware that I had not expected

- An fp32 matmul with two moving columns and a 128x128 stationary operand takes .11 us a pass amid other matmuls, half of a product with 512 columns (.2265).
- GpSimd instructions that follow each other without a pause held two VectorE products one after the other, 5.35 us for 1.42 (after and e12).
- The granted clock behind a gap of TensorE of 5 us cost 1.4 us in one execution and 2.8 in another (0.81 over six microseconds in e12, 0.53 in the kernel after), with the same code around it.
- The clock also fell behind a gap of 2.12 us (0.50 from 1561 to 1564 in the kernel after), and the late tile held ScalarE's take and VectorE's product in turn.
